# A hybrid gated block on one core: the head rebuilt, with the norm's weight row spread by TensorE, loads of x and w_in alternating, and the first token tile in halves

## What is computed

```python
D_MODEL, SEQ, DEPTH = 1024, 512, 1
def hybrid_layer(x, positions, w_in, ...):
    h = rms_norm(x, norm_mix_pre)          # x * rsqrt(mean(x*x) + 1e-6) * norm_mix_pre
    proj = h @ w_in                        # 1024 x 5632: u, v, q, k, v_att, gate_a, gate_b
    u, v_sgu, q, k, v_att, gate_a, gate_b = jnp.split(proj, offs, axis=-1)
    a = chunked_spatial_gating(gelu(u), gelu(v_sgu), ...)
    att = sliding_window_sink_attention(rotary(q), rotary(k), v_att, sinks)
    merged = sigmoid(gate_a) * (a @ w_a) + sigmoid(gate_b) * (att @ w_b)
    x = x + rms_norm(merged @ w_o, norm_mix_post)
    ff = square(relu(rms_norm(x, norm_ff_pre) @ w_ff_in)) @ w_ff_out
    return x + rms_norm(ff, norm_ff_post)
```

## Time and profile before

| | |
|---|---|
| median of 3 runs | 785.18 us (785.15 to 785.74) |
| the profiled execution, time | 785.12 us |
| its span (first to last instruction) | 783.4 us |
| PE (TensorE matmul) busy | 765.7 us, 98% |
| DVE busy | 529.3 us, 68% |
| ACT busy | 365.2 us, 47% |
| POOL busy | 58.4 us, 7% |
| DMA, mean over the span | 102 GB/s |

### The profile page before, as it was taken

How to read it: one execution, slowest core, us unless ns; L and a number is a source line. 1 busy time by engine, 2 the same in 40 slices (tenths; PEclk the granted TensorE clock), 3 DMA queues, 4 the chain that set the end, 5 groups by cost and what they waited for, 6 DMA issues and landing times.

```text
span 783.4 us, 9921 instructions
## 1 busy us (share of the span) xinstructions
PE 765.7 (98%) x3640; PEld 640.7 (82%) x3640; DVE 529.3 (68%) x883; ACT 365.2 (47%) x609; POOL 58.4 (7%) x110
## 2 busy tenths in 40 slices
PE   7999999999999999999999999999999999999994
PEld 6888888888887888888888998888887888878873
DVE  5624667677777336885635779746895579667897
ACT  4522656666565744232325545544443444334542
POOL 3000000022223003000001200000000000000002
PEclk9999999999999999999999999999999999999998
DMA  8333232212132532326331452136003620262002
GB/s 295 109 114 101 70 92 79 83 55 82 55 83 80 188 101 61 114 75 242 107 108 54 161 186 57 54 139 211 27 3 104 259 65 1 56 240 81 0 1 108
DMA packets 91581, 80.29 MB, mean 102 GB/s; under 512 B 2833, under 2 KB 77585, under 8 KB 91537
## 3 DMA queue, kind: packets, MB, share of 16 engines
q1 hardware_dynamic: 90864, 79.70, 31.5%
q10 hardware_dynamic: 672, 0.01, 0.0%
HBM read 77.60 MB, written 2.10 MB: 102 GB/s over the span
## 4 chain that ended last, share of the span: by engine, by line
PE 90%; DVE 6%; ACT 1%; DMA 1%; issue 0%; SPq 0%; POOL 0%; DVEq 0%; POOLq 0%; ACTq 0%
PE acc L1382 26%; PE acc L1384 26%; PE acc L1383 26%; DVE w_lo L1213 2%; PE aux L1383 1%; PE aux L1384 1%; PE aux L1382 1%; DVE sum L1236 1%; DMA w_raw<-in_w_in 1%; PE aux L1569 1%; PE aux L1495 1%; PE aux L1494 1%; PE aux L1504 1%; PE acc L1523 1%; PE acc L1520 1%; PE aux L1477 1%
## 5 line engine op out<-in xcount | busy, mean ns | idle before, releaser
L1382 PE MATMUL acc<-actB_hi,w_hi 128*128 128x512 f32 (+1 forms) x544 | 207.3, 381 | 0.8 <-DVE sum L1318 0.8
L1384 PE MATMUL acc<-actB_hi,w_lo 128*128 128x512 f32 (+1 forms) x544 | 205.4, 378 | 0.0
L1383 PE MATMUL acc<-actB_lo,w_hi 128*128 128x512 f32 (+1 forms) x544 | 205.2, 377 | 0.0
L931 DVE TENSOR_TENSOR w_lo<-w_raw,w_hi 128x1024 fp32r<-128x1024 f32 x72 | 87.8, 1223 | 83.9 <-ACT w_hi L648 83.1
L1382 PEld LDWEIGHTS acc<-actB_hi,w_hi 128*128 128x128 f32 x544 | 102.5, 188 | 19.6 <-DVE w_lo L1209 1.6
L1384 PEld LDWEIGHTS acc<-actB_hi,w_lo 128*128 128x128 f32 x544 | 102.4, 188 | 18.9
L1383 PEld LDWEIGHTS acc<-actB_lo,w_hi 128*128 128x128 f32 x544 | 102.5, 188 | 18.1
L648 ACT ACTIVATE w_hi<-w_raw 128x1024 fp32r<-128x1024 f32 x72 | 75.4, 1052 | 71.1 <-PE acc L1384 68.8
L1382 PE MATMUL acc<-w_hi,actB_hi 128*128 128x512 f32 x160 | 62.7, 392 | 1.5 <-DVE actB_lo L941 1.3
L1384 PE MATMUL acc<-w_hi,op_lo 128*128 128x512 f32 x160 | 63.5, 397 | 0.0
L1383 PE MATMUL acc<-w_lo,op_hi 128*128 128x512 f32 x160 | 63.4, 396 | 0.0
(11 more groups left out here) (192 smaller groups left out, 1292.1 us busy)
## 6 DMA issues: line engine op xcount, KB each, us to landing
w_raw<-in_w_in SPq DMA_DIRECT2D x44, 512.0 KB, 3.9
w_raw<-in_w_ff_in SPq DMA_DIRECT2D x32, 512.0 KB, 4.0
down_raw<-in_w_ff_out SPq DMA_DIRECT2D x16, 1024.0 KB, 6.9
w_raw<-in_w_b SPq DMA_DIRECT2D x8, 512.0 KB, 3.6
w_raw<-in_w_a SPq DMA_DIRECT2D x8, 512.0 KB, 3.5
w_raw<-in_w_o SPq DMA_DIRECT2D x8, 512.0 KB, 3.8
x<-in_x SPq DMA_DIRECT2D x4, 512.0 KB, 7.5
x<-in_x SPq DMA_DIRECT2D x1, 2048.0 KB, 9.0
```

The costliest lines, as they stand in the source:

```text
L931: nc.vector.tensor_tensor(w_lo[:, j], w_raw[:, j], w_hi[:, j].bitcast(F32), ALU.subtract).then_inc(lo_made, 1)
L1382: nc.tensor.matmul(o, a_hi, b_hi, start=first, stop=False)
L1383: nc.tensor.matmul(o, a_hi, b_lo, start=False, stop=False)
L1384: return nc.tensor.matmul(o, a_lo, b_hi, start=False, stop=last)
```

## The change

- SP no longer loads `g_pre`. ACT's queue loads the weights once, as one row of 4 KB on one partition (`g_row`); TensorE multiplies ones by it (two plain float32 matmuls), and ACT copies the result to `g_pre`.
- SP's order of loads is now x0, x1, unit 0, unit 1, x2, unit 2, x3, unit 3.
- Tile 0's epsilon is added within DVE's sum of squares, so POOL does one instruction for it. Its norm, transposes and conversions go in two halves of 512 columns.
- The warm-up has 8 transposes, the spread, then 18.
- The order of conversions on ACT and DVE and of steps on TensorE is new: unit 0 and 1 on tile 0, transposes of tile 1, three steps, transposes of tile 2, its steps with units 0 to 2, transposes of tile 3, its steps with units 0 to 2, and last unit 3 on all four tiles.

```diff
-WARM_UP = 40
+WARM_UP = 26
+WARM_FIRST = 8
...
-T_QK = TT
+T_QK = TT - 1
...
             load_x(1)
-            sp.dma_start(g_pre[:], norm_mix_pre[0:1, :].to_broadcast([P, D])).then_inc(g_pre_in, 16)
-            for j in (0, 1):
-                load_rows(j, w_in_v, 2 * j, slice(C_Q, C_Q + COL))
-            load_x(2)
-            load_x(3)
-            for j in (2, 3):
+            for j in range(SLOTS):
+                if j >= 2:
+                    load_x(j)
                 load_rows(j, w_in_v, 2 * j, slice(C_Q, C_Q + COL))
...
+            nc.gpsimd.memset(ones[:], 1.0)
...
-            for t in range(TT):
-                pool.wait_ge(ssq_act if t else ssq_dve, max(t, 1))
+            pool.wait_ge(ssq_dve, 1)
+            nc.gpsimd.tensor_tensor(rstd[:, 0, 0:1], ssq[:, 0, 0:1], neg_half[:], ALU.pow).then_inc(rstd_made, 1)
+            for t in range(1, TT):
+                pool.wait_ge(ssq_act, t)
                 inv_sqrt(ssq[:, 0, t:t + 1], 0, t, rstd_made)
...
+            act.dma_start(g_row[0:1], norm_mix_pre[0:1, :]).then_inc(g_row_in, 16)
...
-                act.wait_ge(turned, base + t + 1)
+                act.wait_ge(turned, base + t + (1 if base else 0))
...
+            act.wait_ge(g_spread, 1)
+            nc.scalar.activation(g_pre[:], acc[:, 0:2].rearrange("p a n -> p (a n)"), ACT.Copy).then_inc(g_made, 1)
             square(1)
             hi_of(0)
-            turn_hi(0, 0, actB_hi)
+            for h in range(2):
+                act.wait_ge(half_turned, h + 1)
+                nc.scalar.activation(actB_hi[:, 4 * h:4 * h + 4, 0:P], aux[:, h].rearrange("p (k s) -> p k s", s=P),
+                                     ACT.Copy).then_inc(half_hi, 1)
+            hi_of(1)
+            hi_of(2)
             turn_hi(0, 1, actB_hi)
-            hi_of(1)
             square(2)
             square(3)
+            hi_of(3)
             turn_hi(0, 2, actB_hi)
             turn_hi(0, 3, actB_hi)
-            hi_of(2)
-            hi_of(3)
...
-                dve.wait_ge(turned_hi, base + t + 1)
+                dve.wait_ge(turned_hi, base + t + (1 if base else 0))
...
-                                           1.0 / D, 0.0, ALU.mult, ALU.add, ssq[:, 0, 0:1]).then_inc(ssq_dve, 1)
+                                           1.0 / D, EPS, ALU.mult, ALU.add, ssq[:, 0, 0:1]).then_inc(ssq_dve, 1)
...
-            dve.wait_ge(g_pre_in, 16)
-            norm(0)
+            dve.wait_ge(g_made, 1)
+            dve.wait_ge(rstd_made, 1)
+            for h in range(2):
+                cols = slice(h * COL, (h + 1) * COL)
+                nc.vector.scalar_tensor_tensor(x0[:, 0, cols], x0[:, 0, cols], rstd[:, 0, 0:1], g_pre[:, cols],
+                                               ALU.mult, ALU.mult).then_inc(half_normed, 1)
+            lo_of(0, 0)
+            for h in range(2):
+                dve.wait_ge(half_hi, h + 1)
+                at = (slice(None), slice(4 * h, 4 * h + 4), slice(0, P))
+                nc.vector.tensor_tensor(actB_lo[at], aux[:, h].rearrange("p (k s) -> p k s", s=P),
+                                        actB_hi[at].bitcast(F32), ALU.subtract).then_inc(half_lo, 1)
+            lo_of(1, 1)
             norm(1)
-            lo_of(0, 0)
-            turn_lo(0, 0, actB_hi, actB_lo)
+            lo_of(2, 2)
             turn_lo(0, 1, actB_hi, actB_lo)
-            lo_of(1, 1)
             norm(2)
+            turn_lo(0, 2, actB_hi, actB_lo)
             norm(3)
-            turn_lo(0, 2, actB_hi, actB_lo)
+            lo_of(3, 3)
             turn_lo(0, 3, actB_hi, actB_lo)
-            lo_of(2, 2)
-            lo_of(3, 3)
...
-                pe.wait_ge(normed, (TT if base else 0) + t + 1)
-                if t >= 2:
+                pe.wait_ge(normed, TT + t if base else t)
+                if base and t >= 2:
                     pe.wait_ge(turned_lo, base + t - 1)
+                elif t == 2:
+                    pe.wait_ge(half_lo, 2)
+                elif t == 3:
+                    pe.wait_ge(turned_lo, 1)
                 for k in range(KT):
...
+            def warm_up(times):
+                for _ in range(times):
+                    nc.tensor.transpose(acc[:, 3, 0:P], ident[:], ident[:])
+
             pe.wait_ge(pool_consts, 1)
-            for _ in range(WARM_UP):
-                nc.tensor.transpose(acc[:, 3, 0:P], ident[:], ident[:])
-            turn_tile(0, x0, 0)
+            warm_up(WARM_FIRST)
+            pe.wait_ge(g_row_in, 16)
+            for h in range(2):
+                m = nc.tensor.matmul(acc[:, h], ones[:], g_row[0:1, h * COL:(h + 1) * COL], start=True, stop=True)
+            m.then_inc(g_spread, 1)
+            warm_up(WARM_UP - WARM_FIRST)
+            for h in range(2):
+                pe.wait_ge(half_normed, h + 1)
+                for k in range(4):
+                    m = nc.tensor.transpose(aux[:, h, k * P:(k + 1) * P],
+                                            x0[:, 0, (4 * h + k) * P:(4 * h + k + 1) * P], ident[:])
+                m.then_inc(half_turned, 1)
+
+            def first_step(n, t):
+
+                if t == 0:
+                    pe.wait_ge(half_lo, n // 2 + 1)
+                else:
+                    pe.wait_ge(turned_lo, t)
+                pe.wait_ge(lo_made, n + 1)
+                m = rows_step(n, actB, 2 * n, t, n == 0, n == SLOTS - 1)
+                if n == SLOTS - 1 or t == TT - 1:
+                    m.then_inc(pe_done, 1)
+
+            first_step(0, 0)
+            first_step(1, 0)
             turn_tile(0, x0, 1)
-            for n, t in ((0, 0), (0, 1), (1, 0), (1, 1), (0, 2), (1, 2), (0, 3), (1, 3)):
-                pe.wait_ge(turned_lo, t + 1)
-                pe.wait_ge(lo_made, n + 1)
-                m = rows_step(n, actB, 2 * n, t, n == 0, False)
-                if t == TT - 1:
-                    m.then_inc(pe_done, 1)
-                if n == 1 and t < 2:
-                    turn_tile(0, x0, t + 2)
-            for n in (2, 3):
-                pe.wait_ge(lo_made, n + 1)
-                for t in range(TT):
-                    m = rows_step(n, actB, 2 * n, t, False, n == 3)
-                    if n == 3 or t == TT - 1:
-                        m.then_inc(pe_done, 1)
+            for n, t in ((2, 0), (0, 1), (1, 1), (2, 1)):
+                first_step(n, t)
+            turn_tile(0, x0, 2)
+            for n in range(3):
+                first_step(n, 2)
+            turn_tile(0, x0, 3)
+            for n in range(3):
+                first_step(n, 3)
+            for t in range(TT):
+                first_step(3, t)
             with pe.Fori(1, 3) as b:
                 rows_block(actB, b * SLOTS, bank_free=lambda t: pe.wait_ge(acc_to_act, b * TT + (t + 1 - TT)))
```

More of the change, by code:

```diff
@@ L297, in hybrid_block @@
         ident = keep("ident", [P, P])
+        ones = keep("ones", [1, P])
         mask = keep("mask", [P, 2 * P])
@@ L334, in hybrid_block @@
         with ExitStack() as a:
-            x0, _, g_pre, _, qk = group(a, [
-                ("x0", [P, TT, D], F32), ("pad0", [P, 4096], F32), ("g_pre", [P, D], F32), ("pad1", [P, D], F32),
+            x0, _, g_pre, g_row, qk = group(a, [
+                ("x0", [P, TT, D], F32), ("pad0", [P, 4096], F32), ("g_pre", [P, D], F32), ("g_row", [P, D], F32),
                 ("qk", [P, TT, NH, HD], F32)])
@@ L362, in hybrid_block @@
         x_in = [sem(f"x_in{t}") for t in range(TT)]
-        g_pre_in = sem("g_pre_in")
+        g_row_in = sem("g_row_in")
+        g_spread, g_made = sem("g_spread"), sem("g_made")
         consts_in = sem("consts_in")
@@ L384, in hybrid_block @@
         normed = sem("normed")
+        half_normed, half_turned, half_hi, half_lo = (sem(n) for n in (
+            "half_normed", "half_turned", "half_hi", "half_lo"))
         turned, turned_hi, turned_lo = sem("turned"), sem("turned_hi"), sem("turned_lo")
```

## The result

| | before | after |
|---|---|---|
| median | 785.20 us | 795.04 us (794.99 to 795.21, 4 runs) |
| ratio | | 1.0121, 95% interval 1.0109 to 1.0134 |
| span of the profiled execution | 783.4 us | 793.5 us |

The changed kernel is slower by 9.8 us. The direction was the one forecast (+5.5 us, 790.6), the size was not, and the time lies above the range (789.4 to 792.8).

What follows compares the result with a forecast made beforehand. The kernel was taken as bound by TensorE (chain 90% PE). Start −1.7, third transposes +0.9, waits +1.7, two gaps +5.2, earlier idle −0.6 gave +5.5 us on 785.1: 790.6, range 789.4 to 792.8.

Steps and rivals of the forecast that it cites:

- the two gaps: Block 0, ahead of tiles 2 and 3: TensorE waits for each tile's conversion, 2.6 us idle, twice; 5.2 us in the sum.
- the middle: Block 0 from step (1,0) to tile 3: waits of 0.45, 0.25 and 1.0 us, tile 2 starting at 26.3.
- The chain of angles: On DVE after tile 3's remainder: starts at 33.75, first q copy done 43.25, just fits; at most some tenths lost.
- The shorter warm-up (26 for 40) ends ahead of the first half's norm: TensorE's head: warm-up transposes done before tile 0's first half is normed, so no cost; first matmul at 12.05, 1.7 us sooner.
- A second term: The spread, two plain fp32 matmuls on TensorE: 0.9 to 2.0 us, up to 3.9 at the early pace; 2.8 taken.
- The row: The 4 KB weight load, issued at 0.8: lands between 2.8 and 5.2, 3.5 taken.
- Against it: after the 2.2 us of idleness from 7.9 to 10.1: Argument against a clock fall: after that idleness eight transposes took 0.86 us, as eight do later.
- The clock rival: TensorE's clock falls after idling ahead of the first step and in the gaps: 1.5 us each, 792.1 for one; chance 0.12.
- A sign of being wrong: In the profile after: matmuls standing 0.45 us apart after a gap would show the forecast wrong.
- The 795: The clock rival's time for three falls of TensorE's clock, at 1.5 us each; the rival's chance 0.12.
- the 793.1: Rival of a late weight row: landing at 5.2 and slow pace make all 2.5 us later, no start gain; chance 0.05.
- The chain of waits behind it does not go through the norm: Kernel before, first real matmul at 13.76: held by unit 0's load until 10.23, its rounding and remainders, not the norm.

Runs made afterwards that it cites:

- The run with the gaps filled: The changed kernel with 20 transposes of the identity into an unused bank behind the transposes of tile 2 and of tile 3: 792.94 us, ratio 1.0093.
- The rebuilt head: Three kernels with new DVE norm, tile 1's transposes ahead of the first step, order covering conversions, against the kernel before: 787.14 us; row loaded first 783.36; one-row spread 783.71.
- the kernel with the weights by DMA: The changed kernel with TensorE's order altered, g_pre loaded by SP in third place again and 40 warm-up transposes in one piece: 789.05 us, ratio 1.0047.

## Why the prediction was right and wrong

**Right: the two gaps.** The forecast took 3.47 us from a tile's first transpose to its first matmul and got 2.6 us of waiting twice. Measured: 3.41 and 3.40, with 2.37 shown as idle and 2.6 lost from start to start. Moving TensorE's order alone took 6.7 us off. That a matmul of the tile follows its own transposes is the largest cause.

**Right: the middle.** Ahead of tile 1's first step TensorE idled 0.92 (1.0 forecast); from there to tile 2's transposes were 4.22 us (4.08), from there to tile 3's 7.63 (7.55). The chain of angles did not hold TensorE, whose matmuls run on without a break into block 1, and nothing was given back behind block 0.

**Wrong, 2.6 us: "The shorter warm-up (26 for 40) ends ahead of the first half's norm".** This step of the head failed. It costed the 18 transposes behind the spread at nothing, though the same paragraph said that the array is slow at first. At 0.217 us each they took 3.9 us, until 11.37, and tile 0's own took 1.91 for under 1. A second term was too small: the spread took 3.7 us (2.8 taken, 3.9 the upper end), and the rounding of unit 0 started at 9.54 for 9.0. The row had landed by 2.3, for 3.5 taken, and that gained nothing: the eight transposes ahead of the spread ran until 3.8. The first matmul came at 13.84 for 12.05, 1.8 late, and the second half and unit 1 behind it added 0.8: tile 2's transposes started at 25.37 for 22.8. The run with 4 transposes confirms the mechanism and splits the 1.8: its first matmul came at 12.49, so 1.35 are the warm-up's, and the other 0.45 fit the longer spread. It also shows that the gain could not have been had so: the first steps then run at the slow pace.

**Wrong, 1.7 us: "Against it: after the 2.2 us of idleness from 7.9 to 10.1".** The clock rival was priced at 1.5 us a fall and given 0.12. One fall came, behind tile 3's gap, and cost 1.5 us; the last seven steps took 11.27 us for 9.53. The rows of before showed one idle stretch without a fall, and I took it to clear two of 2.6. The run with the gaps filled shows that idleness was the cause. A sign of being wrong that the prediction named, matmuls 0.45 apart after a gap, is there (0.427). The Trainium skill (TensorE: Matmul & The Clock Gate, Part 1) says that the array falls back to half its clock when it idles; this trace agrees, with 0.51 behind the second gap.

Together 2.6 and 1.7 are the 4.3 us between the forecast and the measured end of block 0 (43.35 and 47.67). The range held the fall of the clock alone (790.6 + 1.7 = 792.3). It held neither the late head alone (793.2) nor both. (Its lower end was also added up a little low: 790.6 less 0.7 and 0.3 is 789.6.) That two rivals come near such numbers is luck. The 795 was given for three falls, and one came; the 793.1 was given for a row that lands at 5.2, and the row was early.

**A reading that was too narrow, without a price: "The chain of waits behind it does not go through the norm".** In the kernel before unit 0's landing did end the chain, but DVE had been at work almost without a break since 8.79, so with an earlier unit 0 alone DVE would have come no sooner to its remainder. The run with the spread alone had that landing and gained nothing; there the late transposes stood in the way as well, so it does not prove this by itself. The rebuilt head, in which DVE's norm starts at 6.45, is the one that gained, but it changes more than that.

## What to carry to other kernels

Where one engine transposes and two others convert, put work of another tile between a tile's transposes and its first use, as long as the way through the others takes; count that distance once in a trace, and check the order of instructions against it at each tile. Warm-up work stands in an in-order list like any other: cost it at the pace of a cold array, and put it only where the next real work cannot be ready. A gap can cost twice, its own length and the slower clock that may follow it. Here two gaps of 2.4 us brought one fall of 1.5 us, so repeated gaps of this size belong with a fall of the clock in the forecast itself, not in a rival.

## What the runs showed of the hardware

- The page's granted clock read 1.00 in the whole head, while transposes stood 0.217 us apart there and 0.107 later, and so it did over the slow first matmuls of the run with 4 transposes (12.49 to 17). There the pace is to be read from the distance of the rows. Where the array had reached its fast pace and then fell, in the kernel with the weights by DMA, the column does show it: 0.50 from 13 to 16 us.
- A fall of TensorE's clock came 0.8 us after the gap's end and lasted 3.34 us (granted 0.51, matmuls 0.427 us apart for 0.227); with 4 warm-up transposes it came 1.3 us after, and lasted 3.29. Both times it came behind the second gap of 2.37 us, not behind the first.
- Transposes alone do bring the array to its fast pace: with nothing else on TensorE there were 14 in 3 us and then 28 in the next 3. By the Trainium skill (TensorE: Matmul & The Clock Gate, Part 4: PE-mode transpose) they would not; the measurement decides.
- A plain float32 matmul of 128x512 shows as two records of 0.93 us at the slow pace, 3.7 us for two calls, on one row of the array as on 128; where the pace rose within it, 2.77.
- A load of 4 KB took 1.5 us when issued at 0.79, ahead of the loads of 512 KB. Issued at 2.02, with three loads of 512 KB issued before it, it took over 5: 1.2 us later in the list, 4.9 us later on the chip.
